# Moving every remaining weight low part of a two-block transformer kernel from GpSimd to VectorE

## What is computed

```python
for l in range(2):
    hc = modulate(xc, ...)
    if l == 1:
        mem = context_memory(hc, p)          # keys, values and two scan states only
    else:
        yc, mem = context_mixer(hc, p)       # attention + gated linear attention + convolution
        xc = post(xc, yc, ...)
        xc = post(xc, ffn(modulate(xc), p), ...)
    x = post(x, latent_mixer(modulate(x), mem, ...), ...)
    x = post(x, ffn(modulate(x), p), ...)
for l in range(2):                           # the second block
    y = mixers(rmsnorm(x) @ w_in[l])         # latent attention, short convolution, pooling, window attention
    x = x + mixed(y) @ w_o[l]
    x = x + (silu(gate) * up) @ w_down[l]
return rmsnorm(x)
```

## Time and profile before

| | |
|---|---|
| median of 3 runs | 3313.21 us (3308.41 to 3314.64) |
| the profiled execution's own time | 3308.83 us |
| its span in the trace | 3307.0 us, 57858 instructions |
| mean granted TensorE clock | 0.932 of full speed |
| PE busy | 2991.7 us (90%) |
| DVE busy | 2167.6 us (66%) |
| ACT busy | 1517.5 us (46%) |
| POOL busy | 1051.8 us (32%) |

### The profile page before, as it was taken

One profiled execution on the slowest core, in us unless ns is written; L12 is line 12 of the kernel. 1 busy time (PEld: TensorE's weight loads), 2 busy tenths in 40 slices (PEclk: granted clock), 3 DMA queues, 4 the chain that ended last, 5 costly groups with the idle time before them and its releaser, 6 DMA issues.

```text
span 3307.0 us, 57858 instructions
## 1 busy us (share of the span) xinstructions
PE 2991.7 (90%) x21908; PEld 2832.6 (86%) x21908; DVE 2167.6 (66%) x3271; ACT 1517.5 (46%) x3134; POOL 1051.8 (32%) x646
## 2 busy tenths in 40 slices
PE   6999988999989988889988999889899889998998
PEld 5989878899989977889987999668899869996998
DVE  0766596676677589677645775887657556646655
ACT  1454434444554423444454544234444455554544
POOL 1000000058500000008853000000278627873777
PEclk6889988999999988999989999889899989999999
DMA  5344333435444323335532443224455314541455
GB/s 204 114 142 134 115 115 103 159 128 177 159 134 147 110 98 112 123 107 176 178 111 96 147 152 109 83 71 142 154 175 179 109 52 159 178 153 58 147 167 166
DMA packets 121592, 441.86 MB, mean 134 GB/s; under 512 B 13552, under 2 KB 15600, under 8 KB 120992
## 3 DMA queue, kind: packets, MB, share of 16 engines
q1 hardware_dynamic: 109568, 393.35, 35.9%
q10 hardware_dynamic: 11808, 45.42, 4.0%
HBM read 437.67 MB, written 1.05 MB: 133 GB/s over the span
## 4 chain that ended last, share of the span: by engine, by line
PE 42%; issue 20%; DVE 17%; POOL 14%; ACT 5%; DMA 1%; SPq 1%; POOLq 0%; DVEq 0%; ACTq 0%
POOL w_lo L1014 14%; PE lin L476 9%; PE lin L477 9%; PE lin L478 9%; DVE arena L1728 7%; PE lin L526 4%; DVE w_lo L1585 3%; PE aux L714 2%; ACT w_hi L1049 1%; PE aux L577 1%; PE aux L602 1%; ACT arena L1209 1%; DVE small L1742 1%; DVE s_lo L1666 1%; PE lin L734 1%
## 5 line engine op out<-in xcount | busy, mean ns | idle before, releaser
L1014 POOL TENSOR_TENSOR w_lo<-w_raw,w_hi 128x1024 fp32r<-128x1024 f32 (+1 forms) x642 | 1051.6, 1659 | 2248.8 <-ACT w_hi L1049 2248.5
L476 PE MATMUL lin<-h_hi,w_hi 128*128 128x256 f32 x3584 | 1045.3, 292 | 47.4 <-DVE w_lo L1585 32.1
L477 PE MATMUL lin<-h_lo,w_hi 128*128 128x256 f32 x3584 | 1029.9, 287 | 0.0
L478 PE MATMUL lin<-h_hi,w_lo 128*128 128x256 f32 x3584 | 1028.6, 287 | 0.0
L1049 ACT ACTIVATE w_hi<-w_raw 128x512 fp32r<-128x512 f32 x1446 | 827.8, 623 | 150.9 <-PE lin L476 109.5
L476 PEld LDWEIGHTS lin<-h_hi,w_hi 128*128 128x128 f32 x3584 | 704.7, 197 | 59.7 <-issue 30.7
L477 PEld LDWEIGHTS lin<-h_lo,w_hi 128*128 128x128 f32 x3584 | 704.5, 197 | 0.4
L478 PEld LDWEIGHTS lin<-h_hi,w_lo 128*128 128x128 f32 x3584 | 703.2, 196 | 0.0
L1585 DVE TENSOR_TENSOR w_lo<-w_raw,w_hi 128x1024 fp32r<-128x1024 f32 x315 | 381.1, 1219 | 217.1 <-ACT w_hi L1049 215.8
L476 PE MATMUL lin<-s_hi,w_hi 128*128 128x256 f32 x1392 | 407.8, 293 | 16.9 <-DVE s_lo L1666 7.4
L477 PE MATMUL lin<-s_lo,w_hi 128*128 128x256 f32 x1392 | 400.2, 287 | 0.0
(11 more groups left out here) (252 smaller groups left out, 4280.5 us busy)
## 6 DMA issues: line engine op xcount, KB each, us to landing
w_raw<-in_stream SPq DMA_DIRECT2D x723, 512.0 KB, 3.3
a_raw<-in_ada ACTq DMA_DIRECT2D x80, 512.0 KB, 3.4
arena<-in_ada SPq DMA_DIRECT2D x11, 512.0 KB, 12.9
s_f<-in_ada SPq DMA_DIRECT2D x5, 512.0 KB, 15.8
X<-in_tokens SPq DMA_DIRECT2D x2, 1024.0 KB, 12.2
arena<-in_const ACTq DMA_DIRECT2D x1, 1856.0 KB, 9.5
arena<-in_small ACTq DMA_DIRECT2D x1, 1536.0 KB, 13.6
out<-arena SPq DMA_DIRECT2D x1, 1024.0 KB, 3.9
```

The costliest lines, as they stand in the source:

```text
L476: used(pe.matmul(o, whi, hi[:, k, :], start=k == 0, stop=False), first)
L477: pe.matmul(o, whi, lo[:, k, :], start=False, stop=False)
L478: mm = pe.matmul(o, wlo, hi[:, k, :], start=False, stop=k == kcs - 1)
L1014: ins = pool.tensor_tensor(w_lo[:, slot, part], w_raw[:, slot, part], w_hi[:, slot, part].bitcast(F32), ALU.subtract)
```

## The change

GpSimd's program is deleted. VectorE makes the low part of every load that is used: its `lows` no longer has an upper end per mixer, it is also called in the feed-forward's loop (with counts that contain the loop's register), in the memory pass and in the second block, and its waits for `hi_ready` are given by the place in the loop. The pieces of 256 columns are gone; every low part is one instruction on 1024 columns. `tile_at` is now also written inside the loop. In the memory pass each scan pair is followed by a call of `evac`. Transfers, high parts and matmuls are the same instructions.

```diff
-        @block.gpsimd
-        def _(pool):
-            def low_parts(first, last, pieces):
...
-            low_parts(0, SLOTS, PIECES)
-            for k, load in enumerate(ffn_at):
...
             def lows(load):
-                first, last = low_next
-                for m in range(first, min(load, last)):
-                    dve.wait_ge(sems["hi_ready"], 2 * m + 2)
+                for m in range(low_next[0], load):
+                    dve.wait_ge(sems["hi_ready"], at.value("hi_ready", 2 * m + 2))
                     dve.tensor_tensor(w_lo[:, m % SLOTS, :], w_raw[:, m % SLOTS, :], w_hi[:, m % SLOTS, :].bitcast(F32), ALU.subtract
                                       ).then_inc(sems["lo_ready"], 1)
-                low_next[0] = max(first, min(load, last))
+                low_next[0] = max(low_next[0], load)
+
+            def lows_for(k):
+                lows(tile_at[n.at("lin_evac") + k] // TILES + SLOTS - 1)
 
             def evac(k=1):
-                c = n.up("lin_evac", k)
-                lows(tile_at[c] // TILES + SLOTS - 1)
-                return c
+                lows_for(k)
+                return at.up("lin_evac", k)
...
             def feed_forward(x, scaled):
...
                     for c in range(HALF):
-                        dve.wait_ge(sems["lin_evac"], at.up("lin_evac", 2))
+                        dve.wait_ge(sems["lin_evac"], evac(2))
...
             def gla_memory(l, s):
-                n.up("lin_evac", 4 + len(MEMORY_UNITS[:2]))
-                scans()
-                for u in MEMORY_UNITS[2:]:
-                    unit(l, u)
+                evac(4 + len(MEMORY_UNITS[:2]))
+                scans(lambda c: unit(l, MEMORY_UNITS[2:][c]))
...
                 step(dve.memset(w2["up"][:, :, 0:16], 0.0))
+                lows_for(8)
                 inverse(aux[0], slot=0)
...
-                dve.wait_ge(sems["lin_evac"], at.up("lin_evac", 9))
+                dve.wait_ge(sems["lin_evac"], evac(9))
...
+                lows_for(2)
...
-                dve.wait_ge(sems["lin_evac"], at.up("lin_evac", 4))
+                dve.wait_ge(sems["lin_evac"], evac(4))
...
-                dve.wait_ge(sems["lin_evac"], at.up("lin_evac", 3 + 2 * MH + 2))
+                dve.wait_ge(sems["lin_evac"], evac(3 + 2 * MH + 2))
```

More of the change, by code:

```diff
@@ L58 @@
 SLOTS = 3
-PIECES = 4
 ADA_CHUNKS = 6 * D // P
@@ L465, in done @@
                 mm.then_inc(sems["lin_done"], 1)
-                if at.turn is None:
-                    tile_at[n.at("lin_done")] = max(at.tile, tile_at.get(n.at("lin_done") - 1, 0))
+                tile_at[n.at("lin_done")] = max(at.tile, tile_at.get(n.at("lin_done") - 1, 0))
             def dense(hi, lo, ready=None, kcs=KC):
@@ L1681, in residual @@
                 for c in range(KC):
-                    dve.wait_ge(sems["lin_evac"], evac() if at.turn is None else at.up("lin_evac"))
+                    dve.wait_ge(sems["lin_evac"], evac())
                     dve.scalar_tensor_tensor(x[:, c, :], x[:, c, :], alpha, gate_buf[:, c % 2, :], ALU.mult, ALU.add
@@ L1709, in feed_forward @@
                     at.leave()
+                    assert low_next[0] == low_first + 3 * HALF
+                    low_next[0] += 3 * HALF
                 dve.wait_ge(sems["r_ready"], at.now("r_ready"))
@@ L1984, in _ @@
                         centre(before, early)
+                        evac(KVH + QT + 1)
                         scaled(early, lambda c: v1(pl, "ln2_g", c))
                         n.up("x_ready", KC)
-                        n.up("lin_evac", KVH + QT + 1)
                         inverse(aux[0], ROWS, name="row_ready")
+                        evac(2)
                         heads_normed(heads, {})
-                        n.up("lin_evac", 2)
                         gla_memory(l, s)
@@ L1996, in _ @@
                     y0, pieces = n.at("y_ready"), iter(range(CONV_PIECES))
-                    turns = [k for k, p in enumerate(PASSES) if whole(*p)]
-                    low_next[:] = mixer_at[turns.index(turn)] + SLOTS, ffn_at[turns.index(turn)]
                     for c in range(KC):
-                        if c == 0:
-                            dve.wait_ge(sems["lo_ready"], low_next[0])
                         dve.wait_ge(sems["lin_evac"], evac(2))
```

7 lines of the change are left out of this document (2 added, 5 removed).

## The result

The kernel after takes 3285.26 us (3283.68 to 3286.12, 4 runs) beside 3310.81 us (3307.72 to 3314.64, 4 runs) for the kernel before on the same chip. The ratio is 0.9922, 95% interval 0.9905 to 0.9939. So it is 25.6 us faster, where I had forecast 13.5: the direction was right and the size was not; the time lies 0.3 us above the lower end of the range. The profiled execution took 3283.7 us, with a span of 3281.9.

The account below looks back on a forecast made before the run. TensorE, busy 90% of the span, was taken to set the time. The terms 15.2 + 3.9 + 0.8 + 1.0 - 5.2 - 2.2 gave 13.5 us, so 3299.7 us against the median 3313.2; range 3285 to 3313.

Parts of the forecast that it names:

- the memory pass: Memory pass: 6.6 us of stops and lost clock removed, 4.9 new, 0.7 more lost; net gain 1.0, between -4 and 6.
- the stop in the feed-forward: Before each half's fourth load and before its down chunks: 0.85 us back per stop, twenty stops, 17.0 us.
- The feed-forwards: Ten halves: 17.0 us of stops less 1.75 for late third loads, net 15.2; first low parts behind a feed-forward 0.8.
- the third load's low part: Feed-forward loop, behind the norm's eight low parts: 0.45 us late three times, 0.2 twice, together 1.75 us lost.
- The ends of the output projection: Three ends where the last sum waited for GpSimd: 1.3 us gained at each, 3.9 in all.
- The second block: Twice, from VectorE's queue order: 5.7 us of new stops against 3.1 removed, net loss 2.6 a layer, 5.2.
- 2.2 for the clock: Half clock behind the second block's 3.9 us stop, once a layer: 2.2 us lost, between 0 and 4.4.
- the stop at load 11: Second block: the low part after load 10's stands behind four window sums, a new stop of 1.3 us.
- VectorE's load: Whole run: 494 us of low parts come in, 352 us of standing go; VectorE busy some 2,300 us, 70%.
- More comes back: Rival, 3286 us, chance 0.14: clock does not fall, second block's stops absent, tails give 2.0 each; 14 us more return.
- The slower rival: Rival, 3332 us, chance 0.11: VectorE's queue becomes the limit in the feed-forward's loop, 19 us slower.

Follow-up runs that it names:

- e1: Kernel after, with the low parts of the feed-forwards' loads and the three behind each given back to GpSimd: 3306.45 us, ratio to before 0.9982.
- e10: Kernel after, with one unused GpSimd subtraction for each feed-forward load: 3323.58 us, ratio to before 1.0033.
- e6: Kernel before, with GpSimd making the feed-forward's low parts in four pieces of 256 columns: 3342.02 us, ratio to before 1.0094.
- e2: Kernel after, with the memory pass's loads, from its third to the third of the next mixer, given back to GpSimd: 3293.06 us, ratio to before 0.9946.
- e4: Kernel before, without GpSimd's low parts of the padding loads that are never used: 3309.69 us, ratio to before 0.9993.
- e3: Kernel after, with the second block's loads outside its feed-forwards given back to GpSimd: 3282.48 us, ratio to before 0.9912.
- e5: Kernel after, with two unused GpSimd subtractions of constants for each feed-forward load: 3601.55 us, ratio to before 1.0870.
- e9: Kernel after, with two unused GpSimd copies per feed-forward load, each behind a four-column subtraction: 3301.9 us, ratio to before 0.9965.

## Why the prediction was right in sign and wrong in size

Three terms failed: the memory pass, put at 1.0 us and measured at 5.7; the stop in the feed-forward, put at 0.85 us and measured at 1.00; and the final norm, which had no term and gave 2.4. With 4.7, 2.3 (net of what came late) and 2.4 us they make 9.4 of the 11.6 us between the forecast and the difference of the two traces.

- **The feed-forwards, -15.2 - 0.8 forecast, -18.3 measured.** The mechanism was right at each point (e1). The step that was mis-sized is the price of a stop: 0.75 idle + 0.11 longer start = 0.85, where the distance of starts gives 1.00. Twenty stops make 3.0 us of it. Against that, the third load's low part is 0.6 to 0.9 us late in the first block (forecast 0.45); in the second it is 0.15 (forecast 0.2). The rest lies at the ends of the feed-forwards, and in up to 1.4 us of scatter where the two halves meet.
- **The ends of the output projection, -3.9 forecast, -4.4 measured.** The sum is right by luck: not 1.3 each came, but 3.2 at the first end and 0.5 and 0.7 at the others. Nor was the row at 1446.76 the last sum, which is at 1449.69, and it was not the only one that stood; the norm's last small operation before it took 2.52 us for 0.42:

```profile
1443.74 2.52 DVE L1606 SCALAR_TENSOR_TENSOR rstd<-tmp,rstd 128x256 f32<-128x256 f32 x1
```

  So 4.1 us of standing go there, and two low parts of 1.22 come. In e1 and e10, where GpSimd works there in instructions of 1.3 to 2.5 us, the first end takes 41.0 and 40.8 us, in e6 with its pieces of 0.8 us 37.5.
- **The memory pass, -1.0 forecast, -5.7 measured (e2: 5.5).** This is the largest failure. What goes: the stops at 1743.09 and 1748.07 gave back 2.7 and 2.1 us, the clock behind them 1.5 (I had taken 1.1), and load 13 0.7: 7.0 and not 6.6. What comes: one stop of 3.0 us by starts and 0.5 four loads later, in place of 3.6 + 1.3; and 0.2 ahead of the value chunks in place of 0.7. From load 15 on another 2.5 us went that I had not looked for, among them GpSimd's last stop (0.66) and half a microsecond of the wait for the scan's state (4.8 to 4.3 us). At the pass's start I had the cause right and the outcome wrong: ScalarE's high part for the fourth load is as late as before (12.4 us after the pass's first matmul in both traces), but TensorE does not meet it any more, since it stood before the third load, for the low part behind the centring, and ran at half clock after that. That this cost nothing in the sum was luck.
- **The final norm, no term, -2.4 measured (e4).** I had costed GpSimd's stands only where the stands lay on rows I read: product, difference, rounding, last sum. The last rows of GpSimd's own timeline were not among them.
- **The second block, +5.2 and +2.2 for the clock forecast, +7.3 measured in the trace.** Chain of 7.65 us, stop of 3.74, and the half clock behind it were right; the stop at load 11 was not. That the sum fits is luck: over all traces the stages cost 4.5 us more than with GpSimd, and 2.8 by the medians of e3.
- **VectorE's load, 2,300 us forecast, 2145 measured.** The 494 us came (492 measured); the standing that I had counted (352 us) is only that of three operations in the loop. 22 us less in all means that 514 went: of the other 160 some 96 stood in the residuals, 21 in the sums, and the rest in norms, scans and window sums beside GpSimd.
- **The rivals.** "More comes back" named 3286 us, and 3285 came, but not for its reasons: the clock did fall, and the large stops of the second block were there. The slower rival had the right place (e5 shows that the loop's limit is VectorE once it is held up) and the wrong condition: without GpSimd VectorE is busy 61.2 us of a half's 97.4.

What stays open: the two groups of e9's runs, why the first end of the output projection gained so much more than the other two, and what moving the second block's stages costs to better than 2 us. The 1.3 us in start and mixers are within the scatter: the kernels whose queue there is that of after take 1727.5 to 1734.8 us for them, before and e4 1730.0 and 1729.8.

## What to carry to other kernels

Price a stop by the distance of starts over the usual pace, not by its idle time. When an engine is emptied, go through its own timeline to the last row and ask of each of its instructions who runs beside it: the part that nobody waits for, here two padding loads, costs as much as any other. And before giving GpSimd "free" work beside a VectorE that is half busy, add to VectorE's busy time about 1.0 us for each of GpSimd's instructions (the stand measured in e5) and compare it with the time that TensorE gives. Here that estimate is 61 + 33 = 94 us for a half of 97, and the 33 unused instructions cost 1.2% (38 us); 61 + 66 = 127 us is over it, and 66 cost 9.6% (316 us), with a half of 128.2.

## What the runs showed that I had not expected

In these rows VectorE and GpSimd hold each other up one instruction at a time, and each one's recorded duration contains its stand: 2.26 us for one of 1.29, 1.47 for one of 0.43. So the busy share of the held engine is no measure of its work; VectorE made more low parts in fewer busy microseconds. The price of idle work is far from linear: 38 us for one subtraction a load, with VectorE busy 87% in the loop (78.58 of 90 us), and 316 for two, with 96% (86.36). Nothing between was run. And cutting an instruction to shorten the stand lengthened the chain: four pieces of 0.80 us for one of 2.47 passed TensorE's 2.88 a load and cost 30 us.
